# An order of loads and norms in a two-layer trunk: experts with fixed places, x first, norm 1's squares in the pooling stage

## The reference

```python
cs = jax.nn.silu(c)
for i in range(DEPTH):                                   # 2 layers
    mod = cs @ w_mod[i] + b_mod[i]                       # 9 rows x 6144
    sh1, sc1, g1, sh2, sc2, g2 = jnp.split(mod, 6, axis=-1)
    h = modulate(x, norm_g[i, 0], sh1, sc1)              # rmsnorm * (1 + sc1) + sh1
    mix = pool_mixer(h, ...) if i == 0 else recurrent_block(h, ...)
    x = x + g1[:, None, :] * mix
    h2 = modulate(x, norm_g[i, 1], sh2, sc2)
    x = x + g2[:, None, :] * moe(h2, router_w, router_b, moe_w_gate[i], moe_w_up[i], moe_w_down[i])
```

## Time and profile before

| what | value |
|---|---|
| median of three runs | 1042.4 us (1041.13 to 1044.21) |
| profiled execution | 1042.29 us |
| its span in the trace | 1040.5 us |
| mean granted TensorE clock | 0.912 of full speed |
| PE busy | 867.1 us, 83% of the span |
| DVE, ACT, POOL busy | 297.9, 199.0, 61.8 us |
| chain that ended last | PE 69%, DMA 12%, DVE 8%, ACT 3% |

### The profile page before, as it was taken

The page is one execution under the profiler, slowest core; times in us unless marked ns, Lnnn a source line. Parts: engine busy times, 40 slices in busy tenths (PEclk is TensorE's granted clock), DMA queues, the critical chain, the costliest instruction groups (busy, mean ns, idle before and its releaser), DMA issues.

```text
span 1040.5 us, 14093 instructions
## 1 busy us (share of the span) xinstructions
PE 867.1 (83%) x5770; PEld 446.4 (43%) x5770; DVE 297.9 (29%) x672; ACT 199.0 (19%) x355; POOL 61.8 (6%) x142
## 2 busy tenths in 40 slices
PE   2778777999999998359999999964599999999930
PEld 0433433443333332248887888743244333333210
DVE  2494470110010110363320256065110110010018
ACT  1230511000110000231111851262110000010014
POOL 1000010000011000000000000000101000011000
PEclk9989688999999999659999999967599999999975
DMA  8999989999999999592020000017999999999983
GB/s 272 413 415 422 420 323 418 422 421 420 414 420 420 420 421 375 194 389 86 1 81 1 1 1 1 6 54 277 423 421 406 331 320 408 421 420 420 422 323 145
DMA packets 58834, 311.31 MB, mean 299 GB/s; under 512 B 8173, under 2 KB 11549, under 8 KB 28041
## 3 DMA queue, kind: packets, MB, share of 16 engines
q1 hardware_dynamic: 46416, 278.98, 66.3%
q0 software_dynamic: 6336, 17.83, 4.4%
q10 hardware_dynamic: 6017, 13.58, 3.6%
HBM read 294.68 MB, written 21.28 MB: 304 GB/s over the span
## 4 chain that ended last, share of the span: by engine, by line
PE 69%; DMA 12%; DVE 8%; ACT 3%; issue 1%; SPq 1%; ACTq 0%; PEldq 0%; POOLq 0%; POOL 0%; PEld 0%; DVEq 0%
PE banks L666 27%; PE banks L688 13%; PE banks L862 12%; DMA ring<-in_moe_w_down_dram 5%; PE banks L915 3%; PE banks L907 3%; PE banks L884 3%; PE banks L635 2%; DMA ring<-in_w_mod_dram 2%; ACT hT L989 2%; DMA work<-h_rows,toks 2%; PE banks L589 1%; DVE work L1206 1%; DMA work<-y_rows 1%; SPq L421 1%
## 5 line engine op out<-in xcount | busy, mean ns | idle before, releaser
L666 PE MATMUL banks<-ring,work 128*32 128x512 f32 (+1 forms) x1280 | 240.3, 594 | 2.7 <-DMA hT<-in_moe_w_up_dram 2.7
L688 PE MATMUL banks<-ring,work 128*32 128x512 f32 (+1 forms) x992 | 155.6, 593 | 4.4 <-DMA ring<-in_moe_w_down_dram 4.4
L862 PE MATMUL banks<-hT,ring 128*128 128x272 f32 x512 | 120.8, 398 | 7.4 <-ACTq L365 6.6
L666 PEld LDWEIGHTS banks<-ring,work 128*32 128x32 f32 (+1 forms) x1280 | 72.4, 118 | 115.8 <-issue 113.4
L666 PE MATMUL banks<-work 128*32 128x512 f32 (+1 forms) x592 | 113.6, 594 | 0.8 <-DMA work<-in_moe_w_up_dram 0.8
L862 PEld LDWEIGHTS banks<-hT,ring 128*128 128x128 f32 x512 | 98.5, 193 | 29.3 <-ACTq L365 6.8
L666 PE MATMUL banks<-hT,work 128*32 128x512 f32 (+1 forms) x368 | 92.2, 612 | 1.7 <-DVE work L1549 1.7
L688 PEld LDWEIGHTS banks<-ring,work 128*32 128x32 f32 (+1 forms) x992 | 50.9, 118 | 94.1 <-issue 92.0
L1566 DVE COPY work<-banks 128x512 f32<-128x512 f32 x22 | 15.2, 691 | 218.7 <-PE banks L688 218.7
L553 PE MATMUL banks<-ring,work 128*32 128x512 f32 x384 | 47.9, 638 | 19.4 <-DMA ring<-in_w_mod_dram 19.4
L1558 DVE TENSOR_TENSOR work<-work,banks 128x512 f32<-128x512 f32 x22 | 15.1, 687 | 143.8 <-PE banks L666 143.8
(11 more groups left out here) (256 smaller groups left out, 837.9 us busy)
## 6 DMA issues: line engine op xcount, KB each, us to landing
ring<-in_moe_w_down_dram SPq DMA_DIRECT2D x58, 1024.0 KB, 19.0
ring<-in_w_mod_dram SPq DMA_DIRECT2D x48, 1024.0 KB, 24.1
ring<-in_moe_w_up_dram SPq DMA_DIRECT2D x40, 1024.0 KB, 15.3
ring<-in_moe_w_gate_dram SPq DMA_DIRECT2D x36, 1024.0 KB, 15.4
work<-in_moe_w_up_dram SPq DMA_DIRECT2D x18, 1024.0 KB, 22.5
hT<-in_moe_w_gate_dram SPq DMA_DIRECT2D x14, 1024.0 KB, 16.2
work<-in_moe_w_gate_dram SPq DMA_DIRECT2D x14, 1024.0 KB, 17.9
hT<-in_moe_w_up_dram SPq DMA_DIRECT2D x6, 1024.0 KB, 14.1
```

What stands on the lines that cost most here:

```text
L666: last = pe.matmul(bank[part][c0:c0 + cn, :], xe[b][:, k, c0:c0 + cn], w[:, kk, :], start=(k == 0), stop=(k == DC - 1))
L688: last = pe.matmul(bank[2 + half][c0:c0 + cn, :], hidT[b][:, k, c0:c0 + cn], w[:, kk, half * HALF:(half + 1) * HALF], start=(k == 0), stop ...
L862: last = pe.matmul(bank[2 * (i % 2) + h][:, 0:H2], w[:, k, :], hT[:, k, h * H2:(h + 1) * H2], start=(k == 0), stop=(k == DC - 1))
```

## The change

Seven things are done at once.

1. Experts 0 and 1 always take positions 14 and 15 (`fixed_last` takes the place of the index in the key that DVE sorts by). Their places come first in the tiles, and their 12 pieces are loaded without waiting for the routing (`load_fixed`), in layer 0 as mod(3) and mod(4) leave ring slots, in layer 1 as the recurrent block leaves them.
2. Of `w_mod`'s six batches five are loaded ahead of the experts of layer 0; the last is loaded behind layer 0's last expert weights, ahead of SP's half of the `y_rows` reads. mod(5) stands ahead of the sums' turns on PE, for which silu(c) is kept (`silu_kept`) and put back by DVE.
3. x is loaded first on SP. Its turns, the squares and the root of norm 0 stand ahead of mod(0). The affine step of norm 0 is a stage of its own, five chunks on ACT and three on DVE, with a gate behind it. The loads of router_w and router_b stand behind that gate, ahead of pool_w's.
4. mod(2) stands ahead of the fourth group of the mix (ahead of the third before). mod(3) stands in the experts' front ahead of the turns of h, mod(4) behind the list matmul.
5. The squares of norm 1 are taken by ACT in the pooling stage, behind each add (`mean_pool`), and the root too.
6. h_rows and x_rows get five buffers in the place of two, and the waits for their stores go.
7. The constant `mean_w` is cut to 32 columns.

```diff
-    GROUP_CAPS = [4] * 3 + [3] * 6 + [2] * 7
-    GROUP_OF = [p for p, n in enumerate(GROUP_CAPS) for _ in range(n)]
+    FIXED = 2
+    RANKED = NE - FIXED
+    GROUP_CAPS = [4] * 3 + [3] * 5 + [2] * 5 + [1] + [3] * FIXED
+    PLACE_ORDER = [*range(RANKED, NE), *range(RANKED)]
+    GROUP_OF = [p for p in PLACE_ORDER for _ in range(GROUP_CAPS[p])]
...
+    MOD_ORDER = [0, 1, 2, 3, 5, 4]
+    AHEAD = 5 * SPB
...
+            def load_fixed(l):
+
+                for u in FIXED_LOADS:
+                    p, part, h = u
+                    x = SLOT[u]
+                    if l == 0:
+                        sp.wait_ge(mod_used, MOD_LAST[x])
+                    elif x < 2:
+                        sp.wait_ge(o_added, 2 * DC)
+                    else:
+                        sp.wait_ge(lru_used, max(x // 2 + 1, 4 if x < 4 else 0))
+                    load_piece(l, p - RANKED, 2 * part + h, piece[x], piece_loaded[x])
...
-            load_mod(0, range(0, 2))
             sp.dma_start(xtok, x_prompt[0].rearrange("(j p) d -> p j d", p=P)).then_inc(in_loaded, 16)
-            load_mod(0, range(2, NSL))
+            load_mod(range(NSL))
...
-            load_mod(1, range(NSL))
+            load_mod(range(NSL, AHEAD))
+            load_fixed(0)
             load_moe(0)
             load_overflow(0)
+            load_mod(range(AHEAD, DEPTH * NSL))
             load_second(0)
...
-                    if n == 2:
+                    if n == 3:
                         mod(2)
...
                 mod_turn(2)
-                mod(3)
-                mod_turn(3)
+                mean_pool(1)
                 stage_end(pe, "pe")
...
+            stage_end(act, "act")
+            for c in range(AFFINE_ACT):
+                affine(0, 0, c)
+            stage_end(act, "act")
             act.dma_start(rw[:, :, :], router_w.rearrange("(k p) e -> p k e", p=P)).then_inc(router_loaded, 16)
             act.dma_start(rb[:, :], router_b.partition_broadcast(P)).then_inc(router_loaded, 16)
...
-            mod_rows(0)
-            stage_end(act, "act")
             act.dma_start(pw, pool_w[0].rearrange("g (k p) n -> p g k n", p=P)).then_inc(poolw_loaded, 16)
...
-                mod_rows(2)
-                mod_rows(3)
+                for n, g in enumerate(GROUP_ORDER):
+                    if n == 3:
+                        mod_rows(2)
+                    for m in range(2):
+                        act.wait_ge(mixed_added, 2 * n + m + 1)
+                        act.activation(hT[:, 2 * g + m, 0:S], xT[:, 2 * g + m, 0:S], ACT.Square).then_inc(sq_ready, 1)
+                norm_root(1)
                 stage_end(act, "act")
...
-                    if j >= 2:
-                        act.wait_ge(r[f"rows_stored{j % 2}"], 16 * (j // 2))
```

More of the change, by code:

```diff
@@ L734, in moe @@
                 sample_logits(l)
+                if l == 0:
+                    mod(3)
                 def counts():
@@ L759, in moe @@
                         counts()
+                        if l == 0:
+                            mod_turn(3)
                 def turn_x(js):
@@ L771, in turn_x @@
                             last.then_inc(r["turn"], 1)
-                if l == 0:
-                    mod(4)
-                    mod_turn(4)
-                else:
+                if l == 1:
                     pe.wait_ge(gate_cols_ready, 1)
@@ L790, in moe @@
                 if l == 0:
-                    mod(5)
-                    mod_turn(5)
+                    mod(4)
+                    mod_turn(4)
                 stage_end(pe, "pe")
@@ L838, in moe @@
                     return
+                pe.wait_ge(silu_c, 3)
+                mod(5)
                 for j in range(NT):
+                    if j == 2:
+                        mod_turn(5)
                     w = TW[j]
@@ L924, in lru @@
                 stage_end(pe, "pe")
+            pe.wait_ge(in_loaded, 16 * 2)
+            n = turn_rows(x_groups(), n)
+            pe.wait_ge(turned_out, n)
             mean(0)
+            pe.wait_ge(silu_c, 1)
+            mod(0)
+            pe.wait_ge(state_loaded, 16 * 3)
+            pe.wait_ge(normed, DC)
+            turn_rows(state_groups(), n)
+            mod_turn(0)
+            stage_end(pe, "pe")
             stage_end(pe, "pe")
             pool_mix()
-            mean(1)
+            spread_root(1)
             logits(0)
@@ L1264, in _ @@
             own(dve.tensor_scalar(row_parts[:, 1, :], row_parts[:, 1, :], quarter[:, 0:1], None, ALU.add))
+            own(dve.tensor_copy(fixed_last[:, :], iota_e[:, :]))
+            for e in range(FIXED):
+                dve.memset(fixed_last[:, e:e + 1], 1e5 * (e + 1))
             own(dve.tensor_copy(invcnt[:, :], iota_e[:, 0:16]))
@@ L1317, in norm @@
             def norm(n, layer, which):
[L1318 to L1326 removed]
+                if n > 1:
+                    norm_sums(n)
+                if n > 0:
+                    norm_scale(n)
+                else:
+                    for c in range(AFFINE_ACT, DC):
+                        dve.tensor_scalar(hT[:, c, 0:S], hT[:, c, 0:S], gainT[:, layer, which, c, 0:1],
+                                          shiftT[:, layer, which, c, 0:1], ALU.mult, ALU.add)
                 h = seqs(hT[:, :, S:T])
@@ L1615, in lru @@
             def lru():
+                mod_out(5)
+                gates(1, 0)
+                adaln(1, 1)
+                gates(1, 1)
                 xs = [small[:, :].rearrange("p (c t) -> p c t", c=DC), small2[:, :].rearrange("p (c t) -> p c t", c=DC)]
```

204 lines of the change are left out of this document (126 added, 78 removed).

## The result

The changed kernel takes 1066.93 us (1066.63 to 1070.46) beside 1043.08 us for the kernel before (1041.13 to 1044.21): a ratio of 1.023, with a 95% interval of 1.0211 to 1.0249, or 23.9 us. The forecast was 1065.8. The profiled execution of the changed kernel was the longest of its four, 1070.46 us with a span of 1068.7, so that the differences read from its trace add up to 28.2 us. Which stretch was 4 us shorter in the other three executions the trace doesn't tell.

The account below looks back on a forecast made before the run. Expert and recurrent stages dominate but keep their matmuls; stretches ahead and between decide, the pooling stage with DMA full. 12.4 + 7.5 + 1.8 + 12.1 - 9.5 - 2.8 + 2.0 = +23.5 on 1042.3: 1065.8 us; terms reach 1057 to 1075.

Parts of the forecast that it names:

- Start: Ahead of the pooling stage: with x loaded first, that stage starts near 46 and not at 57.2, 11 us earlier.
- pool_w: Load for the pooling mix: held packet by packet behind the router's loads, it lands at 92, bounds 73 and 102.
- Is q1 still full then? Yes: While pool_w loads: 16 pieces of w_mod keep SP's queue busy to about 98.
- Pooling stage: Mix to norm 1's reciprocal: first group at clock 0.50, reciprocal at 124.5 instead of 112.07, +12.4 us.
- mod(3): Layer 0's expert front: standing ahead of h's turns, with Exp behind, it costs +7.5 us, bounds 7.1 and 14.2.
- Between the layers: After layer 0's last weights: w_mod's last eight pieces and ACT's reads pass ahead of the y_rows finish, +12.1 us.
- the bound of 14.4: Between the layers: upper end of the y_rows delay, up to +14.4 us by the smaller packets of ACT's reads.
- Layer 1's front and the gather: Layer 1 before its tiles: five buffers end the store wait, -9.5 us; gather beside a quieter queue, -2.8 us.
- Tiles: Expert stages: new order of places makes two single-expert tiles mixed; +1.8 us in layer 0, +2.0 in layer 1.
- Only pool_w's own time counts: Rival on the pooling stage: router's packets don't hold pool_w, which lands at 73; time 1047 us; chance 0.10.
- pool_w is in time: Rival: pool_w lands before PE reaches the mix at 60; reciprocal at 91, sum -10.0, 1032 us; chance 0.10.
- Half clock throughout: Rival on mod(3) in the expert front: it runs wholly at half clock, +6.1, 1072 us; chance 0.08.

Follow-up runs that it names:

- pool_w ahead: Changed kernel with pool_w issued ahead of the loads of router_w and router_b on ACT's queue: 1052.78 us, ratio to before 1.0069.
- the kernel before, in halves: Kernel before with pool_w loaded as two DMAs of half the columns, 2048 packets of 512 bytes: 1055.38 us, ratio 1.0108.
- mod(3) behind the counts: Changed kernel with mod(3) moved behind all turns of h and the routing's counts, ahead of the list matmul: 1067.4 us, ratio 1.0219.
- pool_w in time, y_rows first and mod(3) split: Changed kernel; pool_w on SP's queue behind mod(0)'s pieces, y_rows reads before w_mod's last batch, mod(3) half around norm 1's spread, half after the counts: 1023.53 us.

## Why the prediction was right

The path is the one forecast, and each of its large terms stands within 2 us. That the total, 1066.93 for 1065.8, came within 1.1 us is in part luck: in the trace the differences add up to 28.2 us against 23.5, and the other executions, 4 us shorter than the profiled one, brought the median back to the forecast.

**Start.** The pooling stage starts at 46.6; forecast 46. Right.

**pool_w.** Landed at 92.7; forecast 92. The mechanism, packet for packet beside a full queue, is shown: taking the router's packets away gives 18.8 us (pool_w ahead), and 1024 more packets cost 18.4 (the kernel before, in halves). Two sizes in it were off and cancelled. The router's packets passed at 1105 / 20 = 55 per us, not 61, which is 2 us more; and q1 ran down from 88 on and not from 98, so the last of pool_w's packets passed faster than two full queues let them (435 in the 6.7 us from 86 to the landing, 1005 in the 20 us before). The step "Is q1 still full then? Yes" failed: it took pieces 17 to 32 as free to be issued, 16 pieces. The ring has 12 slots, so that piece 29 waits for piece 17, the first of mod(2), and mod(2) stands behind the mix, which waits for pool_w. 12 pieces of 2.5 to 2.8 us from 58 on are used up at 88 to 92, which is when q1 ran down.

**Pooling stage.** The first group ran at 0.50, as taken from rows 11. From the mix to the reciprocal of norm 1 it took 33.6 us, forecast 32.5. With the mix 0.8 later that makes +14.3 in place of +12.4; in the kernels that start the mix earlier the same stretch took 31.8 to 32.7, so this tail is nearly a constant, and the start of the mix decides.

**mod(3).** +7.1, forecast +7.5. It took 8.58 us in the chain, 7.08 and 1.5 for the granted clock, which was 0.50 in its first 2 us (forecast 1), and held Exp, as the step had it. That it pays for itself, by freeing ring slots, the prediction did not see. It would not have changed the sum, but moving the batch away does not win the term back (mod(3) behind the counts: 7.9 us won, 8.6 lost again in the tiles). The link of the chain:

```profile
137.58 8.58 PE banks L597 x64
```

**Between the layers.** +13.4, forecast +12.1; the bound of 14.4 held. The step added up what has to pass behind the last weight: 28.9 us, and 30.2 were measured, 439.46 to 469.66. It did not see that the scatter lands in 9.39 us and not in 3.17; but w_mod's pieces passed meanwhile at 420 GB/s, so this time is no addition to the sum. The 1.3 us that are missing lie where the DMA engines were not full any more: 329 GB/s from 462 to 469.7.

**Layer 1's front and the gather.** -10.0 and -3.5, forecast -9.5 and -2.8. DVE's wait for the list's matmul is 0.85 us now, 11.04 before, as the step said (within 2 us):

```profile
757.96 0.18 DVE L1633 COPY work<-banks 128x21 f32<-128x21 f32 x1 [0.85 <-PE banks L845]
```

**Tiles.** +1.5 and +2.5, forecast +1.8 and +2.0.

**Not in the sum.** +2.9 in all: the gather of layer 0, 0.4, the norm and the recurrent block behind the sums, 1.6, and the tail, 0.9. No experiment was made on them, and their cause stays open.

**The rivals.** "Only pool_w's own time counts" is refuted: pool_w landed at 92.7 and not at 73, and at 74.3 once its load stood ahead. Even then the time was 1053 and not the rival's 1047, 4 us of it by ACT's blocked issue. "pool_w is in time" was priced at 33.5 us and is worth 27 on the reciprocal: the rival let the mix start at 60 and did not ask what pool_w's 1 MB does to mod(1)'s pieces when it comes first. "Half clock throughout" is refuted by the 8.58 us of mod(3).

So the change holds gains that the order of its loads covers: with pool_w in time, y_rows first and mod(3) split it is 20.7 us faster than the kernel before. As written, two small loads ahead of a needed one, eight loads ahead of a needed read and a batch ahead of the routing cost some 43 us against that. How much of the 20.7 us the kernel before would win by such repairs alone was not tried.

## What to carry to other kernels

Beside a full queue, count the packets of a load on another queue, not its bytes, and issue what is needed first ahead of loads with short rows. Before moving a matmul later, look at which buffer it frees and which load waits for that. An issue behind some 2000 packets of its own queue held its engine for 18 to 21 us here, so keep such issues behind copies that somebody waits for.

## What the runs showed of the hardware

- **An issue can block its engine.** On ACT, the issue of a 60 KB store took 18.11 us behind the packets of the router's loads and pool_w, 2176 in all, and that of an 8 KB load 21.31 behind 2048. Elsewhere the same store was issued in 0.37 us (the kernel before) and the same load in 0.60 (the changed kernel). That the queue had no more room is my reading; no run shows where its limit lies.
- **The small packet's size hardly matters beside a full queue**: 1105 with 64 bytes passed in 20 us, 1028 with 512 bytes, 963 with 1 KB, each against about as many of the other queue, most of 8 KB. With the other queue running empty, 1437, most of 512 bytes, passed in 8 us.
- **An indirect scatter's landing went from 3.17 to 9.39 us** when eight 1 MB loads were queued beside it, and back to 3.2 when they were moved behind the reads of y_rows.
